# Gate products and row-maximum spread of two recurrent mixers in single-pass form, decay rows filled up to 128

## The chip, the cores and the metric

The kernel runs on one core of one Trainium2 chip. The metric is the device time of one execution in microseconds (us). TensorE (PE) multiplies, and its weight loads are listed apart as PEld; VectorE is DVE, ScalarE is ACT, GpSimd is POOL, and SyncE (SP) issues the transfers.

## The reference

A sequence of 256 tokens of width 1024 goes through seven sublayers: FFN, mLSTM mixer, FFN, FFN, Mamba-2 mixer, FFN, and a hybrid layer of attention and short convolution. All is float32. What matters here is how both recurrent mixers make their gates and how they spread rows over a matrix:

```python
# mLSTM, per chunk and head
proj = h @ w_in                       # 8 of its columns are the gates
ig, fg = split(gates + b_gate); lf = log_sigmoid(fg)
b = cumsum(lf)
log_d = where(causal, b[:, None] - b[None, :] + ig[None, :], -inf)
m_t = maximum(max(log_d, axis=-1), b + m)
s = (q @ k.T) * exp(log_d - m_t[:, None])
# Mamba-2, per chunk and head
dt = softplus(dt + dt_bias)           # 32 columns of h @ w_in
a = cumsum(dt * A)
w = (C @ B.T) * exp(where(causal, a[:, None] - a[None, :], -inf)) * dt
y = w @ x + exp(a) * (C @ state)
```

## The kernel before, in words

Weights come in units of 128x2048 numbers (1 MB each) into a ring of five buffers. A large product is made of three products of a rounded type (float32r): ACT rounds a unit (`hi`, L537), DVE subtracts to get the rest (`lo`, L1642), and PE multiplies rounded by rounded, rounded by rest and rest by rounded (`three`). The activations are split in the same way into `xhi` and `xlo`; `hf` holds them unsplit. Each engine's work is written out by hand in program order and tied by semaphores; nothing is scheduled by a planner. SP issues its transfers in one row: a unit's load waits until PE has used the ring buffer (`w_used`), and a load for the modulation of later sublayers (`load_ada`) until DVE has used its buffer (`a_used`, set by the operations of L1652).

**mLSTM mixer (n = 1).** PE makes eight half products of the v projection (`first_two`), and between them `gates()`: eight products of the unsplit `hf` (256 tokens) with `mlw_sb` (36 columns: input gates in 0 to 3, forget gates in 32 to 35). Then come two `feature_block`s (q and k), products of 128x128 weights with 256 columns. Meanwhile DVE adds the biases (L1910, L1911), computes the log sigmoid (`log1p`), two scans (L1919, L1921), and L1923 writes the negated running maximum as row 1 of `gt`. PE turns rows into columns (`turn_rows`), and `row_max()` spreads four rows over 128 partitions: a column of `ident[0:4]` repeated 128 times as weights, `gt[0:4, 1]` moving, in float32. DVE adds and masks (L1939, L1941), ACT takes the exponential (L752), DVE multiplies by the scores (`weighted`, L1968), and PE multiplies by v (`head`). ACT also rounds units in between, and DVE does `lo` and `ada` for later ones.

**Mamba mixer (n = 4).** Eight products of `hf` with `mbw_sb` (32 columns) give the step sizes. DVE computes the cumulated decay (L2029 to L2039), fills `sel` (two identity matrices of 32, one under the other) and `arows` (rounded part in rows 0 to 31, rest in 32 to 63, L2042 to L2046). For each of 16 pairs of heads `decay(p)` makes two products of 64 rows (a column of `sel` repeated, `arows` moving) and one bfloat16 product that adds the mask; `decay_masked(p)` adds the other mask; ACT takes exponentials (L846, L855); DVE multiplies (`weights`, L2098); `heads(p)` multiplies by x. Pairs 0 to 9 stand between pieces of the z projection (`z_piece`), pairs 10 to 15 do not. POOL scales x by the step sizes and by D (L485, L492) at that time.

## Time and profile before

| | us |
|---|---|
| median of three runs | 1443.24 |
| lowest and highest | 1440.71 and 1446.42 |
| span of the profiled execution, first to last instruction | 1436.6 |
| PE busy in it | 1412.7 |
| DVE busy | 1013.4 |
| ACT busy | 719.4 |
| POOL busy | 85.1 |
| mean granted clock of TensorE | 0.995 |

The profiled execution's own time is not listed beside its span; what lies around the span (start and end of the program) is in the runs' times and not in the span. PE's products are pipelined and the ends of their records are modelled, so neighbouring records overlap: the cost of a product in a row of products is the distance between two starts, not the duration. A float32 product of the program shows as two records, a float32r product as one.

### The profile page before, as it was taken

How to read it: one execution, taken by the hardware profiler on the slowest of the kernel's cores; microseconds unless marked ns; L12 is line 12 of the kernel's file. 1: busy time of each engine (PE TensorE's matmuls, PEld its weight loads, DVE VectorE, ACT ScalarE, POOL GpSimd, SP SyncE). 2: the span in 40 equal slices, each digit the busy share in tenths (PEclk: the TensorE clock that was granted, in tenths of full speed). 3: DMA queues.
4: the chain of work that ended last, by engine and by line, in shares of the span. 5: the costliest groups of instructions: out<-in, count | busy, mean ns of one | idle time of the engine just before them, and what ended most of it. 6: DMA issues, size and time to landing. Idle time of an engine off the chain costs nothing.

```text
span 1436.6 us, 18540 instructions
## 1 busy us (share of the span) xinstructions
PE 1412.7 (98%) x7578; PEld 1205.4 (84%) x7578; DVE 1013.4 (71%) x1278; ACT 719.4 (50%) x931; POOL 85.1 (6%) x112
## 2 busy tenths in 40 slices
PE   9999999998999999999999999999999999999997
PEld 8788888987888878888789978788888799999886
DVE  5887776987977769777767965678746544653865
ACT  5544456456544365434566676554345645545433
POOL 1000001001000010000100352100000100000000
PEclk9999999999999999999999999999999999999999
DMA  9887865855978849887544412488755454445542
GB/s 384 358 335 296 334 227 192 320 187 201 390 295 314 311 151 347 308 322 300 201 147 164 175 60 88 176 333 337 282 194 201 147 194 174 147 164 189 186 153 116
DMA packets 51396, 337.41 MB, mean 235 GB/s; under 512 B 6720, under 2 KB 9584, under 8 KB 11376
## 3 DMA queue, kind: packets, MB, share of 16 engines
q1 hardware_dynamic: 51312, 336.23, 62.8%
q8 instruction: 60, 0.98, 0.3%
q14 instruction: 24, 0.20, 0.0%
HBM read 335.12 MB, written 1.09 MB: 234 GB/s over the span
## 4 chain that ended last, share of the span: by engine, by line
PE 87%; DVE 5%; ACT 3%; DMA 2%; issue 1%; POOL 1%; SPq 0%; ACTq 0%; POOLq 0%; DVEq 0%
PE ps L1010 84%; DMA raw<-units 2%; PE ps L1228 1%; DVE wlo L1642 1%; DVE hf L2056 1%; ACT whi L537 1%; PE ps L1119 1%; DVE M L1652 0%; ACT hf L618 0%; POOL base L457 0%; PE ps L1491 0%; POOL ssx L458 0%; DVE xlo L1717 0%; DVE wlo L1647 0%; ACT hf L612 0%
## 5 line engine op out<-in xcount | busy, mean ns | idle before, releaser
L1642 DVE TENSOR_TENSOR wlo<-raw,whi 128x2048 fp32r<-128x2048 f32 x212 | 485.4, 2294 | 206.6 <-ACT whi L537 206.3
L1010 PE MATMUL ps<-whi,xhi 128*128 128x512 f32 x1432 | 568.7, 397 | 7.5 <-DVE wlo L1647 1.7
L1010 PE MATMUL ps<-whi,xlo 128*128 128x512 f32 x1432 | 558.7, 390 | 0.0
L1010 PE MATMUL ps<-wlo,xhi 128*128 128x512 f32 x1432 | 558.5, 390 | 0.0
L537 ACT ACTIVATE whi<-raw 128x2048 fp32r<-128x2048 f32 x218 | 416.7, 1914 | 157.5 <-DMA raw<-units 157.5
L1010 PEld LDWEIGHTS ps<-whi,xhi 128*128 128x128 f32 x1432 | 269.3, 188 | 69.7 <-issue 5.3
L1010 PEld LDWEIGHTS ps<-whi,xlo 128*128 128x128 f32 x1432 | 269.1, 188 | 57.8
L1010 PEld LDWEIGHTS ps<-wlo,xhi 128*128 128x128 f32 x1432 | 269.5, 188 | 52.7 <-issue 0.2
L1010 PE MATMUL ps<-xhi,whi 128*128 128x256 f32 x704 | 202.7, 288 | 0.0
L1010 PE MATMUL ps<-xhi,wlo 128*128 128x256 f32 x704 | 199.9, 284 | 0.0
L1010 PE MATMUL ps<-xlo,whi 128*128 128x256 f32 x704 | 199.8, 284 | 0.0
L1652 DVE SCALAR_TENSOR_TENSOR M<-M 128x1024 f32<-128x1024 f32 x160 | 189.3, 1220 | 0.0
L1010 PEld LDWEIGHTS ps<-xhi,whi 128*128 128x128 f32 x704 | 135.7, 193 | 1.2 <-issue 0.7
L1010 PEld LDWEIGHTS ps<-xlo,whi 128*128 128x128 f32 x704 | 135.7, 193 | 0.3
L1010 PEld LDWEIGHTS ps<-xhi,wlo 128*128 128x128 f32 x704 | 135.6, 193 | 0.0
L701 ACT ACTIVATE xhi<-ps 128x512 fp32r<-128x512 f32 x44 | 26.3, 598 | 133.0 <-PE ps L1228 133.0
L457 POOL TENSOR_SCALAR base<-ssx 128x1 f32<-128x1 f32 x28 | 17.6, 628 | 1120.9 <-ACT M L602 781.2
L697 ACT ACTIVATE M<-ps 128x256 f32<-128x256 f32 x88 | 33.3, 382 | 93.0 <-PE ps L1010 90.5
L1851 DVE TENSOR_TENSOR M<-M,ps 128x256 f32<-128x256 f32 x88 | 36.1, 419 | 33.0 <-ACT M L697 33.0
L935 ACT ACTIVATE M<-ps 128x512 f32<-128x512 f32 x28 | 16.7, 597 | 66.0 <-PE ps L1010 65.9
L1857 DVE TENSOR_TENSOR xlo<-ps,xhi 128x512 fp32r<-128x512 f32 x44 | 30.3, 690 | 25.5 <-ACT xhi L701 25.4
L2056 DVE SCALAR_TENSOR_TENSOR hf<-hf,cols 128x253 f32<-128x253 f32 (+2 forms) x72 | 36.5, 548 | 8.1 <-ACT hf L808 7.1
(238 smaller groups left out, 981.4 us busy)
## 6 DMA issues: line engine op xcount, KB each, us to landing
raw<-units SPq DMA_DIRECT2D x218, 1024.0 KB, 4.9
M<-ada_units SPq DMA_DIRECT2D x82, 1024.0 KB, 7.0
M<-units SPq DMA_DIRECT2D x10, 1024.0 KB, 5.0
gp<-gate_rows SPq DMA_DIRECT2D x7, 512.0 KB, 7.3
M<-cvec SPq DMA_DIRECT2D x2, 512.0 KB, 4.5
x<-x_in SPq DMA_DIRECT2D x1, 1024.0 KB, 6.0
ada_a<-ada_units SPq DMA_DIRECT2D x1, 1024.0 KB, 18.5
ada_b<-ada_units SPq DMA_DIRECT2D x1, 1024.0 KB, 22.4
```

What stands on the lines that cost most here:

```text
L457: step(pool.tensor_scalar(base[:, 0:1], a, b, EPS, ALU.add, ALU.add))
L537: act.activation(rounded(u), landed(u), ACT.Copy).then_inc(w_hi, 1)
L697: act.activation(sil[:, t, :], ps[:, bank, 0:FB], ACT.Silu).then_inc(sil_ok[t], 1)
L701: act.activation(xhi[:, 8 + 2 * (i % 4):10 + 2 * (i % 4), :], ps[:, 6, :], ACT.Copy)\
L935: act.activation(hT[:, first + 4 * i + 2 * b:first + 4 * i + 2 * b + 2, :], ps[:, 4 + b, :].rearrange("p (a b) -> p a b", b=SEQ), func)\
L1010: return pe.matmul(out, lhsT, rhs, start=start, stop=stop, skip_group_check=True)
L1119: r = pe.transpose(ps[:, 2 * t + k // 4, (k % 4) * P:(k % 4 + 1) * P], xn[:, t, k * P:(k + 1) * P], ident[:, :])
L1642: dve.tensor_tensor(rest(u), landed(u), rounded(u).bitcast(F32), ALU.subtract).then_inc(w_lo, 1)
L1652: return dve.scalar_tensor_tensor(out=w, in0=w, scalar=1.0, in1=cb, op0=ALU.mult, op1=ALU.mult, accum_out=sums[:, column:column + 1])
L1851: dve.tensor_tensor(g[i % 2][:, t, :], sil[:, t, :], ps[:, bank, FB:2 * FB], ALU.mult)\
L1857: dve.tensor_tensor(xlo[:, j:j + 2, :], ps[:, 6, :].rearrange("p (a b) -> p a b", b=SEQ), xhi[:, j:j + 2, :].bitcast(F32), ALU.subtract).t ...
L2056: r = dve.scalar_tensor_tensor(out=cacc[:, q, sh:SEQ], in0=cin[:, q, 0:SEQ - sh], scalar=cols[:, col:col + 1], in1=cacc[:, q, sh:SEQ], op0 ...
```

## The change

- The weights of the mLSTM gates become 64 columns wide (`mlw_sb`), and a tile `mlw_two` of 128 columns holds their rounded part and their rest side by side; `mbw_two` (64 columns) does so for the Mamba step sizes. POOL makes both in the first FFN sublayer, once the loads have landed. `gates()` and its Mamba counterpart multiply them by `xhi` and then by `xlo`: 16 float32r products instead of 8 float32 ones. The output has the rounded and the rest part on different partitions, and DVE adds them: two copies and two three-operand operations instead of two operations with the bias (mLSTM), one copy more (Mamba).
- `sel` and `arows` have 128 rows instead of 64. POOL clears both at the start and writes the two identities of `sel`; the two casts of L2042 go.
- `row_max()` uses them: DVE writes the rounded part into rows 0 to 3 of `arows` and the rest into rows 32 to 35 (one operation more), and four float32r products of 128 rows replace four float32 products of 4 rows.
- The 32 products of the decays are made with 128 rows. Their number, type and columns stay.
- `mlb_sb` moves out of the shared buffer.

```diff
-        sel = sb("sel", [2 * H_MB, H_MB], F32R)
-        arows = sb("arows", [2 * H_MB, SEQ], F32R)
+        sel = sb("sel", [P, H_MB], F32R)
+        arows = sb("arows", [P, SEQ], F32R)
...
+            pool.wait_ge(S["const"], 4)
+            step(pool.memset(sel[:, :].bitcast(F32), 0.0))
+            step(pool.memset(arows[:, :].bitcast(F32), 0.0))
+            for k in range(2):
+                k_ = slice(32 * k, 32 * k + 32)
+                pool.tensor_copy(sel[k_, :], ident[k_, k_]).then_inc(S["const"], 1)
+                pool.wait_ge(S["const"], 5 + k)
...
+                    if n == 0:
+                        pool.wait_ge(S["mixer_in"], 96)
+                        for j, (w, two, c_) in enumerate(((mlw_sb, mlw_two, 64), (mbw_sb, mbw_two, H_MB))):
+                            pool.tensor_copy(two[:, :, 0:c_], w[:, :, :]).then_inc(S["gate_w"], 1)
+                            pool.wait_ge(S["gate_w"], 2 * j + 1)
+                            pool.tensor_tensor(two[:, :, c_:2 * c_], w[:, :, :], two[:, :, 0:c_].bitcast(F32),
+                                               ALU.subtract).then_inc(S["gate_w"], 1)
+                            pool.wait_ge(S["gate_w"], 2 * j + 2)
...
                     def gates():
-                        pe.wait_ge(S["mixer_in"], 96)
+                        pe.wait_ge(S["gate_w"], 2)
                         for k in range(KT):
-                            r = mm(ps[0:36, 0, 0:SEQ], mlw_sb[:, k, :], hf[:, k, :], start=(k == 0), stop=(k == 7))
+                            mm(ps[:, 0, 0:SEQ], mlw_two[:, k, :], xhi[:, k, :], start=(k == 0))
+                            r = mm(ps[:, 0, 0:SEQ], mlw_two[:, k, :], xlo[:, k, :], stop=(k == 7))
...
-                            mm(ps[:, h, 0:SEQ], ident[0:4, h:h + 1].to_broadcast([4, P]), gt[0:4, 1, :],
+                            mm(ps[:, h, 0:SEQ], sel[:, h:h + 1].to_broadcast([P, P]), arows[:, :],
...
-                        r = mm(ps[0:H_MB, 3, 0:SEQ], mbw_sb[:, k, :], hf[:, k, :], start=(k == 0), stop=(k == 7))
+                        mm(ps[0:2 * H_MB, 3, 0:SEQ], mbw_two[:, k, :], xhi[:, k, :], start=(k == 0))
+                        r = mm(ps[0:2 * H_MB, 3, 0:SEQ], mbw_two[:, k, :], xlo[:, k, :], stop=(k == 7))
...
-                               sel[:, h:h + 1].to_broadcast([2 * H_MB, P]), arows[:, :], start=(j == 0))
+                               sel[:, h:h + 1].to_broadcast([P, P]), arows[:, :], start=(j == 0))
...
-                    step(dve.tensor_scalar(G(1), ps[32:36, 0, 0:SEQ], mlb_sb[32:36, :], None, ALU.add))
-                    mark(dve.tensor_scalar(G(0), ps[0:4, 0, 0:SEQ], mlb_sb[0:4, :], None, ALU.add))
+                    mark(dve.tensor_copy(G(1), ps[96:100, 0, 0:SEQ]))
+                    step(dve.tensor_copy(G(0), ps[64:68, 0, 0:SEQ]))
+                    step(dve.scalar_tensor_tensor(out=G(1), in0=ps[32:36, 0, 0:SEQ], scalar=mlb_sb[32:36, :],
+                                                  in1=G(1), op0=ALU.add, op1=ALU.add))
+                    mark(dve.scalar_tensor_tensor(out=G(0), in0=ps[0:4, 0, 0:SEQ], scalar=mlb_sb[0:4, :],
+                                                  in1=G(0), op0=ALU.add, op1=ALU.add))
...
-                    dve.tensor_scalar(G(1), G(4), -1.0, None, ALU.mult).then_inc(S["ml_rows"], 1)
+                    step(dve.tensor_scalar(arows[0:4, :], G(4), -1.0, None, ALU.mult))
+                    dve.scalar_tensor_tensor(out=arows[32:36, :], in0=G(4), scalar=-1.0, in1=arows[0:4, :].bitcast(F32),
+                                             op0=ALU.mult, op1=ALU.subtract).then_inc(S["ml_rows"], 1)
...
-                    step(dve.tensor_scalar(R(0), ps[0:H_MB, 3, 0:SEQ], mbv_sb[:, 0:1], None, ALU.add))
+                    step(dve.tensor_copy(R(0), ps[H_MB:2 * H_MB, 3, 0:SEQ]))
+                    step(dve.scalar_tensor_tensor(out=R(0), in0=ps[0:H_MB, 3, 0:SEQ], scalar=mbv_sb[:, 0:1],
+                                                  in1=R(0), op0=ALU.add, op1=ALU.add))
...
-                    for k in range(2):
-                        mark(dve.tensor_copy(sel[32 * k:32 * k + 32, :], ident[32 * k:32 * k + 32, 32 * k:32 * k + 32]))
```

On PE, the gates of the mLSTM mixer stood between two half products of `first_two` like this (line numbers are those of the kernel before):

```order
L1010 MATMUL ps<-unit_at_51,xhi 128x512
L1010 MATMUL ps<-unit_at_49,xlo 128x512
L1010 MATMUL ps<-hf,M 36x256 x8
L1010 MATMUL ps<-whi,xhi 128x512
L1010 MATMUL ps<-wlo,xhi 128x512
```

The row with `hf` is the eight gate products.

Now the same place begins like this (L1028 is the same helper in the changed kernel); the pair of rows with `mlw_two` stands eight times before the next `whi,xhi`:

```order
L1028 MATMUL ps<-unit_at_51,xhi 128x512
L1028 MATMUL ps<-unit_at_49,xlo 128x512
L1028 MATMUL ps<-xhi,mlw_two 128x256
L1028 MATMUL ps<-xlo,mlw_two 128x256
L1028 MATMUL ps<-xhi,mlw_two 128x256
L1028 MATMUL ps<-xlo,mlw_two 128x256
L1028 MATMUL ps<-xhi,mlw_two 128x256
```

Eight products of 36 weight columns have become 16 of 128 weight columns, in the same place.

On DVE, the operations that take up these products stood between two `lo` steps before:

```order
L1642 TENSOR_TENSOR wlo<-raw,whi 128x2048
L1910 TENSOR_SCALAR M<-ps,M 4x256
L1911 TENSOR_SCALAR M<-ps,M 4x256
L1912 SCALAR_TENSOR_TENSOR M<-M 4x256
L1642 TENSOR_TENSOR wlo<-raw,whi 128x2048
L1688 TENSOR_SCALAR M<-M 4x256
```

Three operations stand between the two `lo` steps.

Now five operations of 4x256 stand there instead of three (L1662 is the `lo` step, L1708 the first operation of `log1p`):

```order
L1662 TENSOR_TENSOR wlo<-raw,whi 128x2048
L1932 COPY M<-ps 4x256
L1933 COPY M<-ps 4x256
L1934 SCALAR_TENSOR_TENSOR M<-ps,mlb_sb,M 4x256
L1936 SCALAR_TENSOR_TENSOR M<-ps,mlb_sb,M 4x256
L1938 SCALAR_TENSOR_TENSOR M<-M 4x256
L1662 TENSOR_TENSOR wlo<-raw,whi 128x2048
L1708 TENSOR_SCALAR M<-M 4x256
```

Two copies have come in ahead of the two operations with the bias; nothing was moved past a `lo` step.

## Rows read from the trace of the kernel before

**Rows 1.** The page, busy time in us (share) and instructions of each engine.
```profile
PE 1412.7 (98%) x7578; PEld 1205.4 (84%) x7578; DVE 1013.4 (71%) x1278; ACT 719.4 (50%) x931; POOL 85.1 (6%) x112
```

**Rows 2.** Timeline, PE, mLSTM gates: start us, us, engine, line, operation, operands, count.
```profile
233.61 0.61 PE L1010 MATMUL ps<-unit_at,xhi 128*128 128x512 f32 x2
234.06 0.39 PE L1010 MATMUL ps<-unit_at,xlo 128*128 128x512 f32 x1
234.38 3.64 PE L1010 MATMUL ps<-hf,M 128*36 128x256 f32 x16
...
238.29 0.40 PE L1010 MATMUL ps<-wlo,xhi 128*128 128x512 f32 x1
```

**Rows 3.** Timeline, PE, the first and the last of 120 products of 256 columns.
```profile
243.57 0.28 PE L1010 MATMUL ps<-xhi,whi 128*128 128x256 f32 x1
...
257.84 0.28 PE L1010 MATMUL ps<-xhi,wlo 128*128 128x256 f32 x1
```

**Rows 4.** Timeline, PE, the spread of the row maxima.
```profile
261.23 0.28 PE L1010 MATMUL ps<-xhi,wlo 128*128 128x256 f32 x1
261.44 1.99 PE L1010 MATMUL ps<-M,ident 4*128 4x256 f32 x8
...
263.58 0.28 PE L1010 MATMUL ps<-xlo,whi 128*128 128x256 f32 x1
```

**Rows 5.** Windows: stretch, us, busy PE, PEld, DVE, ACT, POOL, granted clock, DMA share, GB/s.
```profile
264.00:265.00 1.00, 1.00 (x10) 1.00 (x10) 0.81 (x3) 0.59 (x1) 0.00 (x0) 0.89 1.02 410
...
268.00:269.00 1.00, 1.00 (x9) 1.00 (x9) 1.00 (x3) 0.37 (x1) 0.00 (x0) 0.90 0.99 418
...
882.00:883.00 1.00, 1.00 (x5) 0.81 (x4) 0.99 (x3) 1.00 (x2) 0.00 (x0) 0.70 0.00 0
```

**Rows 6.** Timeline, DVE in the mLSTM mixer; in brackets its idle time and releaser.
```profile
238.13 0.47 DVE L1910 TENSOR_SCALAR M<-ps,M 4x256 f32<-4x256 f32 x1 [1.45 <-PE ps L1010]
...
246.27 2.29 DVE L1642 TENSOR_TENSOR wlo<-raw,whi 128x2048 fp32r<-128x2048 f32 x1 [1.67 <-ACT whi L537]
...
276.55 1.02 DVE L1968 SCALAR_TENSOR_TENSOR hf<-hf,ps 128x384 f32<-128x384 f32 x2
```

**Rows 7.** Timeline, PE, the first head of the mLSTM mixer.
```profile
277.53 1.46 PE L1010 MATMUL ps<-M,hf 128*128 128x256 f32 x6
```

**Rows 8.** Timeline, PE, Mamba gates.
```profile
734.42 0.39 PE L1010 MATMUL ps<-whi,xlo 128*128 128x512 f32 x1
734.74 3.64 PE L1010 MATMUL ps<-hf,mbw_sb 128*32 128x256 f32 x16
...
738.53 0.28 PE L1010 MATMUL ps<-xlo,whi 128*128 128x256 f32 x1
```

**Rows 9.** Timeline, DVE in the Mamba mixer.
```profile
787.76 2.71 DVE L2056 SCALAR_TENSOR_TENSOR hf<-hf,cols 128x253 f32<-128x253 f32 x6 [5.20 <-ACT hf L808]
```

**Rows 10.** Timeline, PE, one pair of decay heads.
```profile
860.85 0.28 PE L1010 MATMUL ps<-mask,ident 128*128 128x256 bf16 x1
861.07 0.50 PE L1010 MATMUL ps<-arows,sel 64*128 64x256 f32 x2
...
861.62 1.45 PE L1010 MATMUL ps<-M,E_early 128*128 128x64 f32 x12
```

**Rows 11.** Timeline, PEld (weight loads), the same pair.
```profile
861.07 0.29 PEld L1010 LDWEIGHTS ps<-arows,sel 64*128 64x128 f32 x2
...
861.50 1.43 PEld L1010 LDWEIGHTS ps<-M,E_early 128*128 128x128 f32 x12
```

**Rows 12.** Timeline, PE, two waits among the pairs.
```profile
829.96 1.06 PE L1399 MATMUL ps<-ident,M 128*128 128x128 f32 x8 [0.68 <-ACT M L795]
...
875.84 2.82 PE L1010 MATMUL ps<-M,hf 128*128 128x64 f32 x12 [0.88 <-DVE hf L2098]
```

**Rows 13.** Timeline, DVE at pair 7.
```profile
845.66 1.80 DVE L2098 TENSOR_TENSOR E_early<-E_early,cbm 128x768 f32<-128x768 f32 x1
```

**Rows 14.** Timeline, POOL, the first operation after its set-up work.
```profile
9.36 0.30 POOL L457 TENSOR_SCALAR base<-ssx 128x1 f32<-128x1 f32 x1 [6.92 <-ACT M L594]
```

More of the change, by code:

```diff
@@ L182, in build @@
         sm = m(13072, 8, 8)
-        mlw_sb = m(14336, KT, 36)
-        mlb_sb = m(14624, 1)
+        mlw_sb = m(13824, KT, 64)
+        mlw_two = nc.alloc_sbuf_tensor_at("mlw_two", [P, KT, P], F32R,
+                                          offset=first + 4 * (2 * NS * UNIT + 32 * SEQ + 14336))
+        mlb_sb = sb("mlb_sb", [P, 1])
         hfl = hf[:, :, :].rearrange("p a b -> p (a b)")
@@ L201, in build @@
         mbw_sb = sb("mbw_sb", [P, KT, H_MB])
+        mbw_two = sb("mbw_two", [P, KT, 2 * H_MB], F32R)
         mbd_sb = sb("mbd_sb", [P, H_MB])
@@ L228, in build @@
         e_in = [sem(f"e_in{s}") for s in range(EARLY)]
-        names = """x_in rows_in bias_in mixer_in scratch_out bmr_in out_in c_in
+        names = """x_in rows_in bias_in mixer_in gate_w scratch_out bmr_in out_in c_in
             const e_used e_mm m0_ok xt_ok ct_ok sh_ok cols_tr cols_ok c_ok wd_ps wd_ok acc_dve acc_pool
@@ L1365, in _ @@
                     first_two(n)
-                    pe.wait_ge(S["mixer_in"], 96)
+                    pe.wait_ge(S["gate_w"], 4)
                     for k in range(KT):
-                        r = mm(ps[0:H_MB, 3, 0:SEQ], mbw_sb[:, k, :], hf[:, k, :], start=(k == 0), stop=(k == 7))
+                        mm(ps[0:2 * H_MB, 3, 0:SEQ], mbw_two[:, k, :], xhi[:, k, :], start=(k == 0))
+                        r = mm(ps[0:2 * H_MB, 3, 0:SEQ], mbw_two[:, k, :], xlo[:, k, :], stop=(k == 7))
                     r.then_inc(S["mb_gate"], 1)
@@ L1908, in _ @@
                     dve.wait_ge(S["scratch_out"], 16)
+                    dve.wait_ge(S["const"], 6)
+                    dve.wait_ge(S["mixer_in"], 96)
                     dve.wait_ge(S["ml_gate"], 1)
-                    step(dve.tensor_scalar(G(1), ps[32:36, 0, 0:SEQ], mlb_sb[32:36, :], None, ALU.add))
-                    mark(dve.tensor_scalar(G(0), ps[0:4, 0, 0:SEQ], mlb_sb[0:4, :], None, ALU.add))
+                    mark(dve.tensor_copy(G(1), ps[96:100, 0, 0:SEQ]))
[4 more added lines that the diff above has]
+                                                  in1=G(0), op0=ALU.add, op1=ALU.add))
                     dve.scalar_tensor_tensor(out=G(2), in0=G(1), scalar=-1.0, in1=G(1), op0=ALU.mult, op1=ALU.min)\
@@ L1942, in exponent @@
                                                  in1=mask[:, 0:P], op0=ALU.add, op1=ALU.min).then_inc(S["ml_arg"], 1)
-                    dve.wait_ge(S["const"], 4)
+                    dve.wait_ge(S["const"], 6)
                     for h in range(H_ML):
@@ L2380 @@
     cvec = np.concatenate([a["c"].reshape(1, D), a["c_2"].reshape(1, D)])
-    mlw = np.zeros((D, 36), f32)
+    mlw = np.zeros((D, 64), f32)
     mlw[:, 0:4], mlw[:, 32:36] = a["ml_w_in"][0][:, 3072:3076], a["ml_w_in"][0][:, 3076:3080]
-    mlw = mlw.reshape(KT, P, 36).transpose(1, 0, 2)
+    mlw = mlw.reshape(KT, P, 64).transpose(1, 0, 2)
     mbw = a["mb_w_in"][0][:, 5120:].reshape(KT, P, H_MB).transpose(1, 0, 2)
```

## The prediction

> **What bounds the kernel now.** I read the busy times first: PE works 1412.7 of 1436.6 us [rows 1], so time is gained only where PE gets through sooner and nothing else holds the end of that stretch. Then the timelines of PE where the diff touches it, for the distance between starts, and those of DVE and ACT behind it, for who would be late next. Last the windows, for TensorE's granted clock: it is 2.4 GHz except in two stretches inside the kernel, where it falls to 1.2 GHz, and one at its end. The changed products account for some 20 us of PE time, so no large effect is in question; about 0.5% (7 us) is what a measurement of this kernel can tell from no change. All sums are made against the span of 1436.6 us; the median of the runs, 1443.2, is 6.6 us above it, and I carry differences over to that.
>
> **One pass against float32.** 120 float32r products of 256 columns start between 243.57 and 257.84: 14.27 us over 119 distances, 0.12 us each [rows 3]. A float32 product of as many columns is two records, and 16 of them take 3.6 us [rows 2, 8]: 0.45 us a product. Two float32r products thus replace one float32 product at 0.24 for 0.45.
>
> **mLSTM gates, on PE.** From the last product of 512 columns ahead of them (234.06) to the second behind them (238.29) it is 4.23 us [rows 2]. Two products of 512 columns start 0.45 before that, 0.23 each. Afterwards the stretch is 0.23 + 16 x 0.12 + 0.23 = 2.38, as the weights have the same 128 columns as their neighbours. PE gains 1.85 us.
>
> **Spread of the row maxima, on PE.** 261.23 to 263.58 is 2.35 us [rows 4]; afterwards six distances of 0.12, 0.72. PE gains 1.63. Right behind these products of four rows, within the microsecond from 264, the clock falls to 1.2 GHz, and it is back at 2.4 within the one from 268 [rows 5]: 3.4 us at half speed, 1.7 us of work lost. What PE did before the fall was busy by the records, but with 4 of 128 rows; the 128-row products around it ran at 2.4 GHz. I take it that the fall goes with them. In all PE could be 5.2 us earlier here.
>
> **What of it reaches the end.** PE's next partner is DVE. The first head starts at 277.53 [rows 7] and needs L1968, which ends at 276.55 + 1.02 / 2 = 277.06 [rows 6]: only 0.47 to spare. DVE stands still 1.67 us before 246.27 for ACT, which in turn follows PE [rows 6], so this part moves up by the 1.85 of the gates; from there to L1968 DVE is all but continuously busy. It also gets work: two operations of about 0.47 at the gates [rows 6], which disappear in its idle 1.45 and 1.67 us, and one operation of about 0.4 behind the scans, which does not. So DVE reaches L1968 1.85 - 0.4 = 1.45 earlier, and PE gets 1.45 + 0.47 = **1.9 us**. The remaining 3.3 us become a wait of PE for ACT and DVE ahead of the first head. Bounds: 1.4 (an execution in which the clock did not fall had no 0.47 to spare) and 5.2 (nothing holds PE).
>
> **Mamba gates.** 734.42 to 738.53 is 4.11 us [rows 8]. The new weights have 64 columns, and on both sides they meet weights of 128. Where that happens now, the load doesn't overlap the product before it, it stands open: the next product starts 0.32 after one of 512 columns, not 0.23 [rows 8]. So 0.32 + 0.05 + 15 x 0.12 + 0.31 + 0.22 = 2.70, and PE gains 1.4. The 0.05 is half of a 128-column load, which stands open for 0.1 in the pairs below. DVE's additional copy (0.47) is about what it saves on the two casts; it later waits 5.20 us for PE's side [rows 9], so PE is the bound from here on and the **1.4 us** pass. Bounds: 0.9, if each load of the 16 is open, and 1.6.
>
> **Decay rows.** From one mask product (860.85) over two products of 64 rows and the next mask product to the first product of a head (861.62) it is 0.77 us [rows 10] for four products. The load of the 64-row weights starts together with its product, 0.22 behind the mask product, where 128-row weights behind a mask product start at 861.50, with that product's own start and 0.12 ahead of their first use [rows 10, 11]. Full rows next to full rows should run at 0.12 each, 0.48 for the four: 0.29 gained per pair, 4.6 over 16 pairs. *Bounds 0 and 4.6.* Not all of it passes. The first three pairs stand ahead of a wait of 0.68 for ACT, which is busy on its own account [rows 12]; two more only lengthen PE's wait for the multiplication of pair 7 on DVE, which starts at 845.66 and takes 1.80 beside POOL's work [rows 13]; the last five alternate with ACT and DVE up to the wait of 0.88 at 875.84 [rows 12]. Six pairs are left: 6 x 0.29 = 1.7, less 0.1 for ACT, **1.6 us**. By the Trainium skill, page "TensorE: Matmul & The Clock Gate", section "LDWEIGHTS (loading the stationary operand)", a load takes the time of its columns whatever its rows, so the fill would bring 0 here and the sum would be 1.6 us smaller. On the duration no row here speaks against it, but the trace shows different starts [rows 11], which that rule doesn't cover.
>
> **Costs put at nothing.** POOL clears `sel` and `arows` in the 6.92 us in which it waits at the start [rows 14]. It splits the gate weights during the first FFN; it works 85.1 us in all [rows 1] and has nothing else there, PE needs them tens of us later, and DVE, which POOL may slow, has slack there. If that cover were gone it would be some 5 us of POOL. SP's queue keeps its order; one transfer grows from 36 to 64 columns.
>
> **Sum.** 1.9 + 1.4 + 1.6 = 4.9 us: span 1431.7, median 1443.2 - 4.9 = **1438.3 us**, 0.34% less. The terms' bounds give 2.3 to 11.4.
>
> **Rivals.**
> - *The second fall of the clock goes as well.* It comes at about 875.8, at the end of a wait, and lasts until 882.6 (0.70 is the mean of the microsecond from 882) [rows 5, 12]: the 12 products of a head pair take 2.82 us there against 1.45 [rows 10, 12]. If fuller rows in the decays prevent it, 6.8 us at half speed are worth 3.4 more: 1434.9. For it: the decays are 128 instead of 64 rows deep. Against: PE's wait and the narrow products of the heads stand right ahead of the fall, and they stay. 0.15.
> - *DVE does not hold the mLSTM part.* If PE's 5.2 us pass whole: 4.9 + 3.3 = 8.2 us less, 1435.0. Against it stand the 0.47 us. 0.07.
> - *Every load stands open.* The Trainium skill, same page, section "The mechanism" of the part on packing small matmuls, has loads overlap with products in flight only if their row groups differ. As a mechanism of this kernel: each float32r product with 128 weight columns would cost 0.1 + 0.12, the mLSTM gates would gain next to nothing (16 x 0.22 = 3.5 for 3.6), DVE's additional operation would eat the slack, the Mamba gates would gain 0.9 and the decays 0: 1442.3. The 120 products at 0.12 and the load at 861.50 speak against it [rows 3, 11]. 0.05.
> - *Slower: PE runs ahead, waits, and the clock falls more often.* The places are the waits at 829.96, before 847 and at 865.67. Each further fall like the second costs 3.4 us of PE's work; one is outweighed by the gains, from two on (6.8) the kernel is slower, and three make 10.2 - 4.9 = 5.3 us more, 1448.5. For it: the waits get longer. Against: now PE stands for 0.68 at 829.96 without a fall. 0.05.
>
> **How the numbers follow.** The forecast has 0.68. The runs of the unchanged kernel lie 5.7 us apart, so two medians can differ by 2 us for nothing. Range: 1433.5 to 1442.0, which takes in the two fast rivals, the upper bounds short of all at once, and leaves out the slow one and most of the third. Faster by over 0.5% means under 1436.0: both fast rivals for the most part (0.17) and a tenth of the forecast's own case, 0.25. Slower by over 0.5% needs more than 7 us: 0.03. Within 0.5%: 0.72.
>
> **What would show it.** In the changed profile: 16 gate records 0.12 apart; the four row-maximum products 0.12 apart and a granted clock of 1.00 behind them; PE waiting some 3 us ahead of the first head for ACT or L1968; from mask product to head 0.48 instead of 0.77; longer waits at the places named; the clock still falling near 871. The prediction is wrong if PE does not wait ahead of the first head, if the distances in the pairs stay, or if the clock stays up through the Mamba mixer.

## The result, and the profile after

The changed kernel takes 1433.75 us (median of five runs, 1432.04 to 1436.05); the kernel before, over the five runs taken with it, 1440.71. The ratio is 0.9946 with a 95% interval of 0.9930 to 0.9962: 0.54% faster. Forecast were 1438.3 us, 0.34% less, and "within 0.5%" with 0.72. The profiled execution went from a span of 1436.6 to 1431.1 us, 5.5 us less for a forecast of 4.9. The time of an execution is its span plus 1.8 us (1.7 to 1.9) in every run that has both on record. One execution of the kernel before, taken beside run a, lasted 2843.72 us at a granted clock of 1.000 and is in no mean or interval here.

The page of the changed kernel, busy times (to compare with [rows 1]):

```profile
PE 1402.6 (98%) x7574; PEld 1202.8 (84%) x7574; DVE 1015.1 (71%) x1280; ACT 718.2 (50%) x931; POOL 91.0 (6%) x120
```

PE has 10.1 us less to do, POOL 5.9 more; DVE has 1.7 more and ACT 1.2 less.

The timeline of PE around the mLSTM gates, and around the row maxima (columns as in [rows 2]):

```profile
234.61 0.39 PE L1028 MATMUL ps<-unit_at,xlo 128*128 128x512 f32 x1
234.83 0.28 PE L1028 MATMUL ps<-xhi,mlw_two 128*128 128x256 f32 x1
...
236.63 0.28 PE L1028 MATMUL ps<-xlo,mlw_two 128*128 128x256 f32 x1
236.75 0.40 PE L1028 MATMUL ps<-whi,xhi 128*128 128x512 f32 x1
236.98 0.40 PE L1028 MATMUL ps<-wlo,xhi 128*128 128x512 f32 x1
...
260.00 0.63 PE L1028 MATMUL ps<-arows,sel 128*128 128x256 f32 x4
260.46 0.28 PE L1028 MATMUL ps<-xhi,whi 128*128 128x256 f32 x1
```

From the last product ahead of the gates (234.61) to the second behind them (236.98) it is 2.37 us, where it was 4.23 [rows 2] and 2.38 had been forecast. The 16 gate products stand 0.12 apart, and so do the four of the row maxima (0.46 us for all).

What comes of it, on PE and on ACT in the same stretch; the third fence is DVE, ahead of the first head:

```profile
268.74 0.39 PE L1028 MATMUL ps<-whi,xlo 128*128 128x512 f32 x1
272.23 2.31 PE L1028 MATMUL ps<-M 128*128 128x256 f32 x8 [3.10 <-issue]
...
277.97 1.46 PE L1028 MATMUL ps<-M,hf 128*128 128x256 f32 x6
```

```profile
263.75 0.58 ACT L740 ACTIVATE M<-ps 128x512 f32<-128x512 f32 x1
269.73 1.91 ACT L555 ACTIVATE whi<-raw 128x2048 fp32r<-128x2048 f32 x1 [5.41 <-DMA raw<-units]
271.55 0.58 ACT L740 ACTIVATE M<-ps 128x512 f32<-128x512 f32 x1
```

```profile
271.67 2.29 DVE L1662 TENSOR_TENSOR wlo<-raw,whi 128x2048 fp32r<-128x2048 f32 x1 [0.61 <-ACT whi L555]
...
276.17 1.01 DVE L1996 SCALAR_TENSOR_TENSOR hf<-hf,ps 128x384 f32<-128x384 f32 x2
```

The scores (272.23) need the last evacuation of queries and keys on ACT (its copy of them out of PE's output bank, 271.55). That stands in ACT's program behind the rounding of a unit for which ACT waits 5.41 us: the unit had not landed. PE stands for 3.10 us, and the first head starts at 277.97, where it was 277.53 before [rows 7]. In the kernel before, ACT had waited 1.73 us for the same unit, and PE not at all ahead of the scores:

```profile
270.11 1.92 ACT L537 ACTIVATE whi<-raw 128x2048 fp32r<-128x2048 f32 x1 [1.73 <-DMA raw<-units]
271.93 0.58 ACT L722 ACTIVATE M<-ps 128x512 f32<-128x512 f32 x1
```

The windows, four around that wait and four at the end of the Mamba mixer (columns as in [rows 5]):

```profile
264.00:268.00 4.00, 4.00 (x28) 3.70 (x28) 4.00 (x4) 0.33 (x1) 0.00 (x0) 1.00 0.97 360
268.00:272.00 4.00, 1.13 (x5) 0.59 (x4) 3.39 (x11) 2.27 (x2) 0.00 (x0) 1.00 1.02 430
272.00:276.00 4.00, 3.77 (x12) 3.23 (x13) 4.00 (x4) 2.80 (x3) 0.00 (x0) 0.60 1.02 430
...
864.00:868.00 4.00, 3.44 (x30) 3.01 (x28) 3.88 (x5) 2.92 (x10) 3.44 (x2) 1.00 0.00 0
868.00:872.00 4.00, 3.12 (x26) 2.90 (x27) 3.39 (x6) 3.47 (x8) 0.00 (x0) 1.00 0.01 2
872.00:876.00 4.00, 4.00 (x24) 3.71 (x25) 1.29 (x2) 1.68 (x4) 0.00 (x0) 0.70 0.02 4
876.00:880.00 4.00, 4.00 (x17) 3.29 (x16) 3.46 (x8) 4.00 (x8) 0.91 (x2) 0.88 0.00 0
```

The clock no longer falls behind the row maxima (1.00 from 264 on), but it falls behind the wait, from 272.8 to 276.2. Of the 5.0 us that the mLSTM part has gained by PE's big products at 267, 4.9 are gone again at 276. The second fall starts at 873.6 and lasts 3.4 us, where it lasted 6.8 before.

PE at the Mamba gates, then waits among the pairs of decay heads and one pair; the second fence has the weight loads (PEld) at the border of the gates ([rows 8, 10, 12] before):

```profile
733.81 0.39 PE L1028 MATMUL ps<-whi,xlo 128*128 128x512 f32 x1
734.03 0.28 PE L1028 MATMUL ps<-xhi,mbw_two 128*64 128x256 f32 x1
...
735.79 0.28 PE L1028 MATMUL ps<-xlo,mbw_two 128*64 128x256 f32 x1
735.90 0.28 PE L1028 MATMUL ps<-xhi,whi 128*128 128x256 f32 x1
...
844.26 1.55 PE L1028 MATMUL ps<-M,E_early 128*128 128x64 f32 x12 [0.72 <-DVE E_early L2126]
848.17 1.55 PE L1028 MATMUL ps<-M,hf 128*128 128x64 f32 x12 [0.43 <-DVE hf L2126]
...
857.45 0.28 PE L1028 MATMUL ps<-mask,ident 128*128 128x256 bf16 x1
857.49 0.48 PE L1028 MATMUL ps<-arows,sel 128*128 128x256 f32 x2
...
857.93 1.45 PE L1028 MATMUL ps<-M,E_early 128*128 128x64 f32 x12
...
862.13 0.28 PE L1028 MATMUL ps<-mask,ident 128*128 128x256 bf16 x1 [1.00 <-ACT E_early L864]
```

```profile
733.81 0.13 PEld L1028 LDWEIGHTS ps<-xhi,mbw_two 128*64 128x64 f32 x1
734.04 0.13 PEld L1028 LDWEIGHTS ps<-xlo,mbw_two 128*64 128x64 f32 x1
```

The first weights of 64 columns load at 733.81, during the product ahead of them: no load stands open, and the stretch from 733.81 to the second product behind the gates (736.02) is 2.21 us, not 2.70. A pair takes 0.48 us from mask product to head, as forecast.

Shift of PE's big products (512 columns) against the kernel before, both from their span's start: +0.55 at 215, ahead of anything changed; -1.35 behind the gates, -4.49 at 267, +0.43 from 276 on. At 509, where nothing was changed, it goes down by another 0.9; run a, of the same kernel, is 1.1 us later there than this profile. Then -0.60 ahead of the Mamba gates; by the products of 256 columns it is -2.49 behind them and -2.36 at 762; the head of the pair above is at -3.69 (857.93 for 861.62, [rows 10]), and behind the second fall it is -5.52. So the Mamba gates give 1.9 us, the decays 1.3, the end of the mixer with its shorter fall of the clock 1.8, the mLSTM part 0.1, and 1.0 lies where nothing was changed. These five make 6.1, less the 0.55 at the start. The waits for DVE at 844 and 848 are longer (0.72 for 0.33) or new, as the forecast had it for the one.

### The profile page after: what moved, and what is told of

Read it like the earlier page. It is cut to its first block, busy times and chain, and to the rows that moved or that the text cites. A ratio compares the mean times of both kernels' runs of the same rounds, so it can differ in the third digit from the quotient of the medians.

```text
span 1431.1 us, 18545 instructions
## 1 busy us (share of the span) xinstructions
PE 1402.6 (98%) x7574; PEld 1202.8 (84%) x7574; DVE 1015.1 (71%) x1280; ACT 718.2 (50%) x931; POOL 91.0 (6%) x120
## 4 chain that ended last, share of the span: by engine, by line
PE 82%; DVE 9%; ACT 4%; DMA 2%; issue 2%; POOL 1%; SPq 0%; ACTq 0%; POOLq 0%; DVEq 0%
PE ps L1028 79%; DVE wlo L1662 3%; DMA raw<-units 2%; DVE hf L2084 2%; PE ps L1246 1%; ACT whi L555 1%; PE ps L1137 1%; DVE M L1672 0%; POOL ssx L468 0%; POOL base L467 0%; DVE unit_at L1662 0%; ACT hf L636 0%; DVE wlo L1667 0%; PE ps L1511 0%; DVE x L1766 0%
## 5 line engine op out<-in xcount | busy, mean ns | idle before, releaser
L1662 DVE TENSOR_TENSOR wlo<-raw,whi 128x2048 fp32r<-128x2048 f32 x212 | 486.3, 2298 | 204.1 <-ACT whi L555 203.3
L1028 PE MATMUL ps<-whi,xhi 128*128 128x512 f32 x1432 | 569.0, 397 | 6.6 <-DVE wlo L1667 1.7
L1028 PE MATMUL ps<-wlo,xhi 128*128 128x512 f32 x1432 | 559.0, 390 | 0.0
L1028 PE MATMUL ps<-whi,xlo 128*128 128x512 f32 x1432 | 558.8, 390 | 0.0
L1028 PEld LDWEIGHTS ps<-whi,xhi 128*128 128x128 f32 x1432 | 269.6, 188 | 68.5 <-issue 4.9
L1028 PEld LDWEIGHTS ps<-whi,xlo 128*128 128x128 f32 x1432 | 269.3, 188 | 57.9
L1028 PEld LDWEIGHTS ps<-wlo,xhi 128*128 128x128 f32 x1432 | 269.8, 188 | 52.7 <-issue 0.2
L1028 PE MATMUL ps<-xhi,whi 128*128 128x256 f32 x704 | 201.9, 287 | 0.1
L1028 PE MATMUL ps<-xhi,wlo 128*128 128x256 f32 x704 | 199.1, 283 | 0.0
L1028 PE MATMUL ps<-xlo,whi 128*128 128x256 f32 x704 | 199.1, 283 | 0.0
L1028 PEld LDWEIGHTS ps<-xhi,whi 128*128 128x128 f32 x704 | 135.0, 192 | 0.7 <-ACT hf L826 0.3
L1028 PEld LDWEIGHTS ps<-xlo,whi 128*128 128x128 f32 x704 | 135.0, 192 | 0.3
L1028 PEld LDWEIGHTS ps<-xhi,wlo 128*128 128x128 f32 x704 | 134.9, 192 | 0.0
```

What stands on the lines that cost most here:

```text
L1028: return pe.matmul(out, lhsT, rhs, start=start, stop=stop, skip_group_check=True)
L1662: dve.tensor_tensor(rest(u), landed(u), rounded(u).bitcast(F32), ALU.subtract).then_inc(w_lo, 1)
```

## The experiments

One execution of each kernel could not settle how much of this was chance: the clock falls at other places in other executions. So I sort the time of the runs in two. Span times (1 - mean granted clock) is the **loss at 1.2 GHz**; span times clock is the **rest**. The clock is on record with three digits, so the loss of a single run is known to 0.7 us, and means are worth more. The loss of every kernel also holds 1.0 to 2.5 us from a low stretch that each profile has at its very end, where PE has no work left. The rest comes out too small where PE was not the bound during a fall: over the 103 runs of the kernel before, a run with 1 us more loss is only 0.73 us longer [0.68, 0.78]. Intervals are 95%, from resampling the runs; "changed" is the mean over the 17 runs of the changed kernel (five of the result, twelve of run a), "before" that over 103 runs of the kernel before, taken beside the runs of all experiments. Runs a to h, i to l and m to p were taken on three different chips; the runs of the kernel before beside them have a rest of 1430.3 to 1430.5 us on each and a loss of 8.4 to 10.0.

| kernel | runs | mean us | against changed | loss | rest |
|---|---|---|---|---|---|
| before | 103 | 1441.2 | +6.7 [5.6, 7.7] | 9.0 | 1430.4 |
| changed (with a) | 17 | 1434.5 | | 4.8 | 1427.9 |
| b, decays of 64 rows | 12 | 1439.9 | +5.3 [3.3, 7.3] | 9.1 | 1429.0 |
| c, Mamba gates in float32 | 12 | 1436.3 | +1.8 [0.2, 3.3] | 5.4 | 1429.1 |
| d, mLSTM part as before | 12 | 1435.7 | +1.2 [-0.1, 2.5] | 4.4 | 1429.5 |
| e, 128-row decays alone | 12 | 1436.9 | +2.3 [0.9, 3.8] | 4.2 | 1430.9 |
| f, 128 rows, loads open | 12 | 1438.7 | +4.1 [2.6, 5.6] | 5.4 | 1431.5 |
| g and k, mLSTM reordered | 12 | 1432.9 | -1.7 [-3.1, -0.2] | 5.6 | 1425.5 |
| h, products in the waits | 6 | 1434.6 | 0.0 [-1.1, 1.2] | 3.8 | 1429.0 |
| i, decays of 32 rows | 12 | 1441.0 | +6.5 [4.8, 8.1] | 11.6 | 1427.6 |
| j, decays of 96 rows | 12 | 1436.4 | +1.8 [0.1, 3.5] | 7.4 | 1427.2 |
| l, reordered, mLSTM float32 | 6 | 1434.7 | +0.2 [-1.6, 1.9] | 4.8 | 1428.2 |
| m, full rows in pairs 10 to 15 | 12 | 1436.6 | +2.1 [1.1, 3.0] | 6.7 | 1428.1 |
| n, full rows in pairs 0 to 9 | 12 | 1440.0 | +5.5 [3.3, 7.6] | 11.2 | 1427.1 |

Of the 6.7 us between before and changed, 4.2 [3.0, 5.4] are loss and 2.5 [2.0, 3.1] are rest. At 0.73 us of time for each us of loss, an estimate, some 3.1 come from the clock and 3.6 from PE's work. The 6.7 us are 0.46% of the time; the first five runs showed 0.54%.

**a, the changed kernel again.** No edit.

> The changed kernel once more, beside the three that undo a part of it. Theory A (sum of parts, as the two traces read): the profiled executions differ by 5.5 us, of which the mLSTM part gives 0 (its 4.9 us are lost in a wait of PE for ACT ahead of the scores and in a stretch of 3.4 us at 1.2 GHz that follows it), the Mamba gates 2.0, the decays 1.5, and a second stretch at 1.2 GHz that is 3.4 us long instead of 6.8 gives 1.7; the same shifts should be seen again at the same places, and a median of 1433 to 1435. Theory B (the clock): the number of stretches at 1.2 GHz differs from execution to execution by chance, and what the medians show beyond 3.5 us is that; then this profile may show two or none at other places, and span plus lost clock time (span times granted clock) will be steadier over the runs than the span.

Median 1434.44, ratio 0.9959 [0.9944, 0.9975]. Its profile, with a span of 1437.3, has other falls than the first: none behind the mLSTM wait, but 6.8 us at 828.8 and 6.8 us at 876.6. Theory B holds for the place of the falls; theory A holds for the wait ahead of the scores. PE waits 3.00 us ahead of the scores here too:

```profile
274.20 1.55 PE L1028 MATMUL ps<-M 128*128 128x256 f32 x8 [3.00 <-issue]
278.76 1.56 PE L1028 MATMUL ps<-M,hf 128*128 128x256 f32 x6 [0.24 <-DVE hf L1996]
```

Where the clock does not fall behind that wait, it is DVE's L1996 that holds the first head at last (0.24).

**b, decays of 64 rows.**

```diff
-   sel[:, h:h + 1].to_broadcast([P, P]), arows[:, :], start=(j == 0))
+   sel[0:64, h:h + 1].to_broadcast([64, P]), arows[0:64, :], start=(j == 0))
```

> The changed kernel with 64 rows in the decay products again. Both theories: 0.77 instead of 0.48 us from the mask product to the head of a pair. Theory A: of 4.6 us of PE work 1.5 reach the end, so it is 1.5 us longer up to the last pairs, and the fall of the clock behind them, if it has nothing to do with the rows, stays at 3.4 us: 1435 to 1436. Rival C (fuller rows shorten the fall): the fall is 6.8 us again, and the time 1436.5 to 1437.5.

Median 1439.59, ratio to before 0.9990 [0.9969, 1.0010]: without this one part nearly nothing is left of the gain. The rest is 1.0 us [0.3, 1.8] longer, about as theory A has it, but the loss is 4.3 us [2.1, 6.6] larger. Rival C holds, with more than it had claimed: the median is above its range of 1436.5 to 1437.5. b's profile has a fall of 6.8 us at 876.5, and one of 6.8 behind the mLSTM wait, at 272.3.

**c, Mamba gates in float32.**

```diff
-   mm(ps[0:2 * H_MB, 3, 0:SEQ], mbw_two[:, k, :], xhi[:, k, :], start=(k == 0))
-   r = mm(ps[0:2 * H_MB, 3, 0:SEQ], mbw_two[:, k, :], xlo[:, k, :], stop=(k == 7))
+   r = mm(ps[0:H_MB, 3, 0:SEQ], mbw_sb[:, k, :], hf[:, k, :], start=(k == 0), stop=(k == 7))
```

> The changed kernel with the Mamba gates as eight float32 products. Theory A: PE's big products behind the gates start 2.0 us later against those ahead of them (4.11 us for the stretch instead of some 2.1), and all of it passes, since PE is the bound up to the decays: 1435.5 to 1436.5. Rival D (DVE holds that stretch, its second operation at the gates eats the gain): under 1 us, 1434 to 1435.

Median 1435.64; the big products behind the gates start 1.9 us later than with the change, and 0.45 of it is gone again at 762. In the runs it is 1.8 us [0.2, 3.3], of which 1.2 are rest [0.5, 1.9]. That is near theory A (2.0), but the interval does not shut out rival D (under 1).

**d, mLSTM part as before** (gate products from `mlw_sb` and `hf`; row maxima from `ident[0:4]` and `gt[0:4, 1]`; DVE's operations for them as before).

```diff
-   mm(ps[:, 0, 0:SEQ], mlw_two[:, k, :], xhi[:, k, :], start=(k == 0))
-   r = mm(ps[:, 0, 0:SEQ], mlw_two[:, k, :], xlo[:, k, :], stop=(k == 7))
+   r = mm(ps[0:36, 0, 0:SEQ], mlw_sb[:, k, 0:36], hf[:, k, :], start=(k == 0), stop=(k == 7))
...
-   mm(ps[:, h, 0:SEQ], sel[:, h:h + 1].to_broadcast([P, P]), arows[:, :],
+   mm(ps[:, h, 0:SEQ], ident[0:4, h:h + 1].to_broadcast([4, P]), gt[0:4, 1, :],
```

> The changed kernel with the mLSTM gates and the spread of the row maxima in float32 as before, all else as changed. Theory A: the first head of the mLSTM mixer starts at the same distance from the mixer's beginning as with the change, within 0.5 us, and the time is that of the changed kernel within 1 us, 1433 to 1435. Rival E (the forecast, the gates' 1.9 us pass and only this one execution lost them): 1.9 us more, 1435 to 1436.5.

Median 1435.39. In the profile PE is 1.9 us later behind the gates and 1.6 more behind the row maxima, the 3.5 forecast. Its wait ahead of the scores is the shorter for it:

```profile
275.42 1.55 PE L1028 MATMUL ps<-M 128*128 128x256 f32 x8 [1.45 <-issue]
279.97 0.48 PE L1028 MATMUL ps<-M,hf 128*128 128x256 f32 x1 [0.26 <-DVE hf L1989]
```

In the mean of the runs 1.2 us [-0.1, 2.5] are left. It lies between theory A (0) and rival E (1.9), and the interval does not shut out either.

The profiles of all runs say more. I take the distance from the last product of 512 columns ahead of the gates to the first head. Where the clock falls nowhere in the mLSTM mixer, it is 42.1 to 42.5 us with the changed mLSTM part (a, f, i, j) and 43.5 to 44.1 with the float32 one (d, e and p, a second profile of the kernel before): 1.5 us apart in the mean. The unit for which ACT waits is rounded 1.5 us earlier too (35.0 to 35.5 us behind the same product, for 36.5 to 37.0), and in both groups DVE's product with the scores, which comes behind its own work on that unit, holds the head at last, as here in p:

```profile
278.66 1.56 PE L1010 MATMUL ps<-M,hf 128*128 128x256 f32 x6 [0.24 <-DVE hf L1968]
```

With a fall of 3.4 us at 264 or 265, as in the two other profiles of the kernel before, the distance is 43.5: that fall costs nothing at the head. With one of 3.4 us behind the wait, at 273 to 275, it is 43.1 to 43.9 with the changed mLSTM part (the first profile, c, h, m, n), 1.2 us more than without. So the change gives 1.5 us here, and in the first profile a fall at a costly place took 1.2 of them.

**e, 128-row decays alone** (c and d together undone, the rest as changed).

> The decays of 128 rows alone: both mixers' gates and the row maxima in float32 as before. Over 12 runs each, the mean granted clock times the span was 1430.5 us for the kernel before, 1428.3 for the changed one and 1429.0 with 64-row decays, and the rest of the mean span, lost at 1.2 GHz, was 9.0, 4.7 and 9.1 us. Theory C (full rows in the decays keep the clock up): the loss is 4 to 5.5 us here too, the rest 1430 or a little under, so a median of 1435.5 to 1437. Rival F (a low clock depends on several narrow stretches, the gates and row maxima among them): the loss stays above 7 us and the median above 1438.

Median 1436.84, ratio 0.9964 [0.9948, 0.9980]. Loss 4.2 us, 4.8 less than before [3.4, 6.1]; rest 1430.9, 0.4 above that of before [-0.3, 1.1]. Theory C holds, rival F falls: this part alone brings 4.3 us [3.0, 5.6] of the 6.7. By this split all of it is the clock; at 0.73 us for each us of loss, some 3.5 are (an estimate), and 0.8 would be the shorter pairs.

**f, 128 rows, with loads that stand open.**

```diff
+   mm(ps[:, 2 + p % 2, 0:2], sel[0:64, 0:1].to_broadcast([64, P]), arows[0:64, 0:2], start=True)
    for j in range(2):
```

> The changed kernel with a product of 64 rows and 2 columns ahead of each pair of decays, which should make loads stand open again while the decays keep 128 rows: some 0.2 to 0.3 us more per pair than the 0.48. Theory C (the rows themselves): the loss at 1.2 GHz stays 4 to 5.5 us of the mean span, only the direct cost of 0.5 to 1.5 us comes back, median 1435 to 1436. Rival G (it is the length of a pair, with its stalls of the load, that takes the clock down): the loss is 8 to 9.5 us and the median 1438.5 to 1440.

The pair is 0.88 us, longer than the 0.77 of before:

```profile
857.14 0.28 PE L1028 MATMUL ps<-mask,ident 128*128 128x256 bf16 x1
857.36 0.70 PE L1028 MATMUL ps<-arows,sel 64*128 64x2 f32 x3
...
858.02 1.45 PE L1028 MATMUL ps<-M,E_early 128*128 128x64 f32 x12
```

Median 1438.47, above theory C's range of 1435 to 1436 and at the lower end of rival G's. What tells them apart is the split: loss 5.4 us, 0.6 above changed [-1.0, 2.1] and 3.7 below b [1.4, 6.1]; rest 3.5 longer, where 0.5 to 1.5 were expected. So it is the rows of the decays and not the length of the pair that keep the clock up (rival G falls). The direct cost of the additional products and their open loads, 16 x 0.40 = 6.4 us, passes by half, more than I had thought.

**g and k, the mLSTM mixer reordered.** ACT's evacuation goes ahead of the rounding that waits for a transfer; DVE's `weighted(0)` and `weighted(1)` go ahead of one pass over the modulation weights.

```diff
-   hi(u0 + 10)
    wait_bank(1, u0 + 6, j0 + 1)
    ev_qk(1, 1)
+   hi(u0 + 10)
...
    lo(u0 + 10)
-   ada(v + 4)
    dve.wait_ge(S["ml_E"], 1)
...
    weighted(1)
+   ada(v + 4)
```

> The changed kernel with the last evacuation of queries and keys on ACT ahead of the rounding of the unit that still lands, and on DVE the first two weighted heads ahead of one pass over the modulation weights. Theory A (ACT waits for a transfer, and the evacuation that PE needs waits behind it): the scores start some 2.5 us earlier, the first head some 2 to 3.5 us earlier, and part of it reaches the end: 1431 to 1433. Rival H (the next wait takes it, on DVE or for the transfer of a later unit): the first head is earlier, but by the end of the mixer nothing is left, 1434 to 1435.

> The reordered mLSTM mixer once more, beside the next one: 1431.5 to 1433, 2.4 us under the changed kernel, with no fall of the clock between 265 and 280.

Medians 1432.06 and 1433.61, ratios 0.9929 [0.9905, 0.9953] and 0.9946 [0.9927, 0.9966]; together 1.7 us [0.2, 3.1] less than the changed kernel and 8.3 [7.0, 9.7] less than before. It is the fastest version of the study. In g's profile PE has no wait ahead of the scores, and stands 1.22 us for DVE instead (the second fence is ACT's):

```profile
269.78 1.47 PE L1028 MATMUL ps<-M 128*128 128x256 f32 x8
275.24 1.56 PE L1028 MATMUL ps<-M,hf 128*128 128x256 f32 x6 [1.22 <-DVE hf L1995]
```

```profile
267.23 0.60 ACT L740 ACTIVATE M<-ps 128x512 f32<-128x512 f32 x1 [2.08 <-PE ps L1028]
270.48 1.91 ACT L555 ACTIVATE whi<-raw 128x2048 fp32r<-128x2048 f32 x1 [2.65 <-DMA raw<-units]
```

The evacuation follows PE at once, the unit lands as late as it did. From the last product of 512 columns ahead of the gates to the first head it is 39.8 us (40.0 in k), for 42.1 in run a, and 43.4 in the first profile with its fall. The clock does not fall between 265 and 280 in either profile. Theory A's account of the wait is shown; the expected 2.4 us under the changed kernel were 1.7, and k's median lies above its range. The edits on ACT and on DVE were not tried apart.

**l, the same with the mLSTM part in float32** (the edits of d on top of g).

> The reordered mLSTM mixer with its gates and row maxima in float32 as before. Theory A (the change's mLSTM part is lost in the wait that the reordering removes): now it passes in part, so this one is 2 to 3.5 us longer than the run beside it, 1434 to 1435.5. Rival K (DVE's chain holds the first head whatever PE does): within 1 us of it, 1432 to 1433.

Median 1434.56, in the mean 1.8 us [-0.1, 3.7] above g and k. In the profile the distance to the first head is 42.0 us, for 39.8 and 40.0: once the wait is gone, some 2.1 us of the 3.5 pass, where it is 1.5 with the wait. The runs alone don't quite tell it from nothing.

**h, products in the waits.** 23 repeats of a decay product into a bank about to be overwritten, at the waits of the pairs.

```diff
+   again(p, {2: 3, 7: 4, 8: 3, 14: 4, 15: 1}.get(p, 0))
    for j in range(2):
...
    decay(p + 2)
+   else:
+       pe.wait_ge(S["mb_E"], p + 1)
+       again(p, 4)
    heads(p)
```

> The changed kernel with 128-row products repeated into a bank about to be overwritten, where PE waits in the Mamba mixer (23 of them, 0.12 us each, 2.7 us in all, of which 2.2 lie in waits). Theory C': the two places at which the clock still falls, near 829 and 875, are those waits; filled, the loss at 1.2 GHz goes from 4.7 to under 3 us and the median is 1433 to 1434. Rival: the clock falls as often, and the time is 0 to 1 us longer, 1434.5 to 1435.5.

Median 1435.08. The profile has no fall left in the Mamba mixer; the loss is 1.0 us smaller [-0.3, 2.2] and the rest 1.0 longer. What the clock gives, the products take back: theory C' had expected a loss under 3 us and a median of 1433 to 1434, and the median is in the rival's range.

**i, decays of 32 rows, and j, of 96.** As b, with 32 and 96 in place of 64. i leaves out the product of the rounding's rest in the decays.

> The changed kernel with decays of 32 rows: the products of the rounding's rest are left out (rows 32 to 63 of sel and arows), so decays carry float32r rounding; a pair is 0.77 us as with 64 rows. Theory C (rows of work keep the clock up): the loss at 1.2 GHz is at least the 9.1 us of 64 rows, 9 to 11, and the median 1439.5 to 1441.5. Rival J (any step between full rows and fewer does the same, as a stall would): as 64 rows within 0.5 us, loss 9.1.

> The changed kernel with decays of 96 rows: loads at the border of 96 and 128 rows stand open or not as the trace will show. Theory C: a loss between the 4.7 of 128 rows and the 9.1 of 64, 5.5 to 8 us, median 1436 to 1438.5. Rival J: if the pair takes 0.77 us again, the loss is that of 64 rows, 9.1, and the median 1439 to 1440.

Medians 1441.80 and 1436.13. The loss is 11.6, 9.1, 7.4 and 4.8 us for 32, 64, 96 and 128 rows. The pair, on PE, is 0.77 us with 64 rows (profile of b; 0.76 with 32, profile of i) and 0.48 with 96 (profile of j):

```profile
858.25 0.28 PE L1028 MATMUL ps<-mask,ident 128*128 128x256 bf16 x1
858.47 0.50 PE L1028 MATMUL ps<-arows,sel 64*128 64x256 f32 x2
...
859.02 1.45 PE L1028 MATMUL ps<-M,E_early 128*128 128x64 f32 x12
```

```profile
858.78 0.28 PE L1028 MATMUL ps<-mask,ident 128*128 128x256 bf16 x1
858.82 0.48 PE L1028 MATMUL ps<-arows,sel 96*128 96x256 f32 x2
...
859.26 1.45 PE L1028 MATMUL ps<-M,E_early 128*128 128x64 f32 x12
```

The two effects come apart. The length of the pair has two values, with a step between 64 and 96 rows. The loss follows the rows instead: 96 rows and 128 have the same pair and differ by 2.6 us of loss [1.1, 4.1]. The steps from 32 to 64 rows (2.5 us [-0.1, 5.2]) and from 64 to 96 (1.7 [-0.6, 4.1]) are not shown one by one; from 32 to 96 it is 4.2 [2.2, 6.4]. Theory C holds for j; for i its loss and median were somewhat above its ranges. Rival J's case for i (as 64 rows, 9.1) is unlikely but not shut out, and its condition for j, a pair of 0.77, did not arise.

**m and n, full rows in one part of the pairs.**

```diff
+   n_ = P if p >= 10 else 64
    mm(ps[:, 2 + p % 2, j * SEQ:(j + 1) * SEQ],
-      sel[:, h:h + 1].to_broadcast([P, P]), arows[:, :], start=(j == 0))
+      sel[0:n_, h:h + 1].to_broadcast([n_, P]), arows[0:n_, :], start=(j == 0))
```

For n the condition is `p < 10`.

> The changed kernel with full rows in the decays of pairs 10 to 15 only, 64 rows in pairs 0 to 9. Theory L (the rows matter where the clock falls, at the narrow tail from 860 on, where no big products lie between the pairs): the loss at 1.2 GHz stays near the 4.8 us of the changed kernel, under 6, and the median is 1434.5 to 1436. Rival M (the rows work all through the mixer, or ahead of the first heads): the loss is 7 to 9 us, median 1437 to 1440.

> The reverse, full rows in pairs 0 to 9 and 64 in 10 to 15. Theory L: the loss is near the 9.1 us of 64 rows throughout, 8 to 10, median 1438 to 1440. Rival M: 5 to 7 us, median 1435 to 1437.5.

Medians 1436.27 and 1439.57; n is 3.4 us [1.4, 5.5] longer than m though it has full rows in ten pairs and m in six. Its loss, 11.2, is no smaller than that of 64 rows throughout; m's, 6.7, is 2.4 [0.1, 4.8] smaller. The tail is where the rows matter most. m's loss and median lie between the ranges of theory L and rival M, so some of it is open: the loss of m is 1.9 us [0.5, 3.3] above that of changed, which would be the rows of pairs 0 to 9. n's profile shows what a bad execution can be, in the windows of the tail:

```profile
860.00:864.00 4.00, 3.44 (x25) 2.81 (x23) 2.08 (x2) 3.54 (x12) 2.85 (x3) 0.92 0.53 221
864.00:868.00 4.00, 4.00 (x20) 3.59 (x20) 3.56 (x4) 0.55 (x2) 3.98 (x2) 0.50 0.00 0
...
876.00:880.00 4.00, 4.00 (x21) 4.00 (x21) 2.25 (x3) 2.49 (x3) 0.00 (x0) 0.50 0.02 6
880.00:884.00 4.00, 4.00 (x16) 3.60 (x16) 0.15 (x1) 1.76 (x5) 0.00 (x0) 0.52 0.00 0
```

PE is busy all along, at half speed, for 20.5 us from 863.4; against the first changed profile, PE's big products are 0.4 us later ahead of it and 7.1 behind it. i's profile has the same stretch from 865.5. PE had waited 0.56 us at 862.67; the changed kernel waits longer there (1.00 at 862.13, above), and its clock stays up until 873.6.

**o and p, the kernel before, profiled twice more.**

> The kernel before, one look. 23 of its 80 runs have a mean clock of 0.991 or less, which is 25 us or more at 1.2 GHz; the profiled one had 0.995. If this look meets one of them, theory C expects one long stretch, near 20 us, from about 865 to 875 on, as 32 rows showed it; the rival, falls at new places, three or more of 3.4 or 6.8 us outside the Mamba mixer.

> As the look before it, a second chance to meet an execution with a mean clock of 0.991 or less; otherwise a fall of 6.8 us near 876 and at most one of 3.4 to 6.8 near 265 or 829 are expected.

Mean clocks 0.995 and 0.996: neither is one of the executions with a clock of 0.991 or less. o has falls of 3.4 us at 263.9, 830.5 and 878.3, p one of 6.8 at 877.2. So the places are the known three, and their number and length vary.

A clock of 0.991 or less stands in 29 of 103 runs of before, in 2 of 12 of b, 7 of 12 of i and 6 of 12 of n; in none of 24 runs of j and m, and in none of 89 with full rows in every decay pair (changed, c to h, k, l). Without those 29 the loss of before is 6.7 us instead of 9.0. That they contain the stretch of 20.5 us is inferred: the profiles of n and i, which have it, have 0.990 and 0.991; no profile of before shows it.

## Why the prediction was wrong

The signs that I had named came: the distances, the wait ahead of the first head, the 0.48 of a pair, a fall near 871. The profiled span came out at 5.5 us less for 4.9 as well. That was partly luck, since the parts behind it differ: the mLSTM part gave 0.1 for 1.9, the shorter second fall and the last pairs 1.8, and 1.0 came from a place where nothing was changed. In the means of the runs the change is worth 6.7 us.

- **The step that failed is the one that left the second fall of the clock in place.** The first rival had it ("if fuller rows in the decays prevent it"), with 0.15, because the wait and the narrow heads right ahead of the fall stay. They do stay, and the clock does fall there still (in run a's profile for 6.8 us, as before), but for less time on the average, and in no run with full rows was the clock as low as with the stretch of 20 us. The sum had 1.6 us for the decays, all from the shorter pairs, and nothing for the clock. Run e gains 4.3 us [3.0, 5.6] by the decays alone, with 4.8 us less loss than before, and b, without the full rows, has 4.3 us [2.1, 6.6] more loss than changed. The rival's price, 3.4 us, was near. I had asked whether the fall goes or stays in the one profile; the runs needed how often and how long.
- **The base was another.** I carried 4.9 us over to a median of three, 1443.24; 103 runs have a median of 1440.5. The "6.6 us above the span" were chance too: an execution is its span plus 1.8, and the profiled one (some 1438.4) was one of the better. With so few runs the spread itself, 5.7 us, was the hint: over the 103 runs most of it goes with the loss. So the forecast stood 2.7 us too high before any step of the change; with 1440.5 as its base it would have said 1435.6.
- **Gates and row maxima on PE.** 1.85 and 1.63 us were forecast; run d measures 1.9 and 1.6. This part of the sum was right.
- **What of the mLSTM part reaches the end.** Forecast 1.9, in the first profile 0.1, in the profiles without a fall 1.5, in the runs 1.2 [-0.1, 2.5]. Where the clock does not fall, DVE holds the head at last, as forecast, but the first holder is ACT's evacuation behind a rounding that waits for its transfer, and both move with the landing of that unit. I had seen that PE would wait "for ACT and DVE"; I had not asked what stands ahead of the evacuation in ACT's program. Nor does the fall of the clock "go with" the four-row products: d, e, l and p have them and no fall there, and six profiles of the changed mLSTM part (the first, b, c, h, m, n) have one behind the wait.
- **Mamba gates.** Forecast 1.4, measured 1.9 in the profiles and 1.8 [0.2, 3.3] in the runs, 1.2 of it rest. The weights of 64 columns don't stand open; the row I had argued from is that of float32 weights of 32 columns. The Trainium skill, page "TensorE: Matmul & The Clock Gate", section "The mechanism", lists a load as overlapping products in flight only where the row groups differ, though it also names a background weight buffer as a way. The load at 733.81 has all the rows of the product it overlaps, so the trace speaks against differing row groups as the only case.
- **Decays, directly.** 0.48 for 0.77 us a pair is as forecast, 1.3 by the timeline for a forecast of 1.6; run b has 1.0 of rest. The same page of the Trainium skill, section "LDWEIGHTS (loading the stationary operand)", has the rows change nothing in a load's time. The durations bear that out nearly (0.18 to 0.19 us with 64 rows, 0.19 to 0.20 with 128); what changes is whether the load is hidden, and 96 rows are enough for it.
- **The slower rival** (PE runs ahead and waits, and the clock falls more) named the waits at 829.96, before 847 and at 865.67. The new fall of the first profile is at another wait, at 272.8; that of run a, at 828.8, is at the first of them, where o, of the kernel before, has one too. In sum the rival had no price: the loss went down by 4.2.

## What to carry to other kernels

Take the granted clock of every run, not of the profiled one alone, and split the time into the loss at the lower clock and the rest before arguing about the parts: here one part moved the first by 4 us, and for the others only a move of the second is shown. Where PE's work is narrow and stretches of large products are missing, more rows in a product cost no time here and kept the clock up more of the time; in this kernel the last pairs were worth most. And when PE gets earlier, read the next wait down to the program order of the engine that releases it: two lines exchanged on ACT and one moved on DVE brought 1.7 us more.
